# Row lists of the first two experts made from the ranks, ahead of the rest of the routing

## The reference

```python
def hier_moe(h, w_rg, b_rg, w_re, b_re, w_gate, w_up, w_down):
    t = h.reshape(b * s, d)
    p_group = jax.nn.softmax((t @ w_rg + b_rg).astype(F32), axis=-1)
    pg_top, g_top = lax.top_k(p_group, 1)                     # 1 of 4 groups
    ...
    pe_top, e_top = lax.top_k(p_exp, EXPERT_TOP_K)            # 2 of the 4 experts in it
    pe_top = pe_top / jnp.sum(pe_top, axis=-1, keepdims=True)
    ...
    for gi in range(N_EXPERT_GROUPS):
        hid = jax.nn.silu(jnp.einsum('nd,edf->nef', t, w_gate[gi])) * jnp.einsum('nd,edf->nef', t, w_up[gi])
        y = y + jnp.einsum('nef,efd->nd', hid * combine[:, gi, :, None], w_down[gi])
```

## Time and profile before

| | |
|---|---|
| median of 3 runs | 825.15 us |
| lowest of them | 824.24 us |
| profiled execution, its own time | 824.05 us |
| its span, first to last instruction | 822.1 us |
| mean granted TensorE clock | 0.917 of 2.4 GHz |
| TensorE busy | 679.0 us, 83% of the span |
| VectorE busy | 333.1 us, 41% |
| ScalarE busy | 180.4 us, 22% |
| GpSimd busy | 134.4 us, 16% |
| moved by DMA | 178.26 MB, mean 217 GB/s |

### The profile page before, as it was taken

One profiled execution on the slowest core, in us unless ns is written; L12 is line 12 of the kernel. 1 busy time (PEld: TensorE's weight loads), 2 busy tenths in 40 slices (PEclk: granted clock), 3 DMA queues, 4 the chain that ended last, 5 costly groups with the idle time before them and its releaser, 6 DMA issues.

```text
span 822.1 us, 9279 instructions
## 1 busy us (share of the span) xinstructions
PE 679.0 (83%) x3561; PEld 393.8 (48%) x3565; DVE 333.1 (41%) x752; ACT 180.4 (22%) x434; POOL 134.4 (16%) x176
## 2 busy tenths in 40 slices
PE   0469899999999998889998922999999979999610
PEld 0455445667675797556554522444454434333200
DVE  4932475867567433767312257011211121112007
ACT  3203324122121213446311121111121120111003
POOL 8670022304041273000000001000000000000021
PEclk9769999999999998989999955899999998999865
DMA  9899902222220303540331296189999999999945
GB/s 333 270 309 281 365 17 103 103 103 103 103 103 1 54 1 121 171 172 2 136 120 52 107 389 223 58 279 330 390 389 391 399 387 399 371 380 397 406 130 228
DMA packets 89631, 178.26 MB, mean 217 GB/s; under 512 B 19602, under 2 KB 24300, under 8 KB 89580
## 3 DMA queue, kind: packets, MB, share of 16 engines
q1 hardware_dynamic: 79152, 155.31, 52.8%
q0 software_dynamic: 4544, 16.26, 6.0%
q10 hardware_dynamic: 5884, 6.00, 2.2%
HBM read 159.20 MB, written 18.35 MB: 216 GB/s over the span
## 4 chain that ended last, share of the span: by engine, by line
PE 64%; DVE 15%; DMA 8%; SPq 6%; ACT 3%; issue 2%; POOL 1%; POOLq 0%; ACTq 0%; DVEq 0%
PE ps L1003 11%; PE ps L1114 7%; PE ps L2168 6%; DMA gu<-in_w_up 6%; PE ps L2135 5%; PE ps L1034 4%; SPq L887 3%; PE ps L997 3%; DVE acc L1794 3%; PE ps L2246 2%; PE ps L2252 2%; PE ps L2132 2%; SPq L890 2%; PE ps L1029 2%; PE ps L2159 2%
## 5 line engine op out<-in xcount | busy, mean ns | idle before, releaser
L1003 PE MATMUL ps<-gu,xgT 128*128 128x512 f32 x256 | 116.5, 615 | 9.1 <-DMA gu<-in_w_up 6.5
L1003 PEld LDWEIGHTS ps<-gu,xgT 128*128 128x128 f32 x256 | 49.9, 198 | 71.9 <-issue 64.6
L1460 POOL DMA_INDIRECT xg<-xn_rows,list x16 | 14.9, 932 | 400.2 <-PE ps L972 210.0
L2168 PE MATMUL ps<-hT,winr 128*128 128x512 f32 x144 | 72.5, 612 | 0.2
L1794 DVE SCALAR_TENSOR_TENSOR acc<-ada,st,acc 128x512 f32<-128x512 f32 x84 | 68.1, 811 | 2.3
L1034 PE MATMUL ps<-dn,hidT 128*128 128x512 f32 x128 | 56.5, 594 | 0.0
L1114 PE MATMUL ps<-wout,yT 128*128 128x512 f32 x128 | 55.9, 595 | 0.0
L1082 DVE TENSOR_TENSOR hidm<-sg,ps 128x512 f32<-128x512 f32 x8 | 5.5, 688 | 120.8 <-ACT sg L1050 120.8
L1648 POOL TENSOR_TENSOR cc<-low,lev 128x512 f32<-128x512 f32 x20 | 30.2, 1519 | 129.7 <-DVE low L1980 104.2
L997 PE MATMUL ps<-gu,xgT 128*32 128x256 f32 (+1 forms) x384 | 45.2, 464 | 7.2 <-DMA gu<-in_w_up 7.2
L2135 PE MATMUL ps<-hT,wind 128*128 128x512 f32 x96 | 42.3, 593 | 0.0
(11 more groups left out here) (405 smaller groups left out, 1039.7 us busy)
## 6 DMA issues: line engine op xcount, KB each, us to landing
gu<-in_w_gate SPq DMA_DIRECT2D x16, 2048.0 KB, 18.8
gu<-in_w_up SPq DMA_DIRECT2D x16, 2048.0 KB, 23.5
dn<-in_w_down SPq DMA_DIRECT2D x16, 2048.0 KB, 21.0
ada<-in_w_ada SPq DMA_DIRECT2D x12, 2048.0 KB, 10.0
expert_rows<-zero POOLq DMA_DIRECT2D x12, 512.0 KB, 12.3
expert_rows<-yo ACTq DMA_DIRECT2D x8, 512.0 KB
wout<-in_w_out SPq DMA_DIRECT2D x1, 3072.0 KB, 10.9
x<-in_x SPq DMA_DIRECT2D x2, 1024.0 KB, 6.3
```

Of the source, the lines that this page charges most:

```text
L1003: ins = nc.tensor.matmul(PS[2 * b + w][:, :], T["xgT"][:, k, :], w_in[:, w, k, :], start=(k == 0), stop=(k == KT - 1))
L2168: ins = t.matmul(bank[:, :], w(k), T["hT"][:, k, :], start=(k == 0), stop=(k == KT - 1))
```

## The change

It makes the row lists of experts 0 and 1 in another way, and moves work around them.

- As soon as `rank` is copied, `r16 = (rank + 1) * chosen` is made, and from it, for each of experts 0 and 1, one one-hot matrix of all four token blocks at once (128 x 512 elements; the row number plus 1 equals r16). Four products with one column each (the token's number) per expert make the list. This takes place after the rank products on TensorE and in front of the copy of `count` on DVE.
- DVE copies the two columns of the list behind `order` (the new step `first_list`), and does the block that makes `experts` straight after it. Then comes the rest of the chain as before, up to `r16` (now written over).
- POOL starts on step `first_list`, not `list`; the wait for `list` comes before the gather of expert 2.
- TensorE does rows 0 and gate and up 0 before the 16 list products, and these write to another bank, PS[5], at columns 64 to 91. A wait for `list` stands before down 0, which writes that bank too.
- DVE does `dve_rows(0)` in the middle of the chain (behind line 1366), then the rest of the places, then waits for the 16 list products, copies the list, and does the product of expert 0 and `dve_rows(1)`. The weights w1, w2 and the list of the extra places come after that.

The whole diff:

```diff
--- before.py
+++ after.py
@@ -48,8 +48,9 @@
 FT = F // P
 EXTRA = 12
 NBUF = 3
-ROUTING = {"chosen": 1, "places": 2, "slots": 3, "list": 4, "experts": 5, "w12": 6, "route_i": 7}
-ROUTING_PE = {"rank_mm": 1, "list_mm": 2}
+ROUTING = {"chosen": 1, "first_rows": 2, "second_rows": 3, "first_list": 4, "experts": 5, "places": 6, "slots": 7,
+           "list": 8, "w12": 9, "route_i": 10}
+ROUTING_PE = {"rank_mm": 1, "first_list_mm": 2, "list_mm": 3}
 SIZES = [128] * 8 + [64] * 4 + [32] * 4
 TILE_START = [sum(SIZES[:n]) for n in range(E + 1)]
 TILE_START += [TILE_START[E] + P * (n + 1) for n in range(EXTRA - 1)]
@@ -1175,16 +1176,21 @@
                            start=False, stop=(i == ST))
         ins.then_inc(sem("routing_pe"), 1)
 
+        for e in range(2):
+            pe.wait_ge(sem("routing"), ROUTING[("first_rows", "second_rows")[e]])
+            for i in range(ST):
+                ins = t.matmul(PS[5][:, e:e + 1], T["in_row"][:, e, i, :], T["tok"][:, i:i + 1], start=(i == 0),
+                               stop=(i == ST - 1))
+        ins.then_inc(sem("routing_pe"), 1)
+
+        pe_rows(pe, 0, 0, 16)
+        pe_gate_up(pe, 0, 0)
         pe.wait_ge(sem("routing"), ROUTING["places"])
         for n in range(2):
             for i in range(ST):
-                ins = t.matmul(PS[6][:, P:P + E + EXTRA], T["in_row"][:, n, i, :], T["in_tile"][:, n, i, :],
+                ins = t.matmul(PS[5][:, 64:64 + E + EXTRA], T["in_row"][:, n, i, :], T["in_tile"][:, n, i, :],
                                start=(n + i == 0), stop=(n == 1 and i == ST - 1))
         ins.then_inc(sem("routing_pe"), 1)
-
-        pe.wait_ge(sem("routing"), ROUTING["list"])
-        pe_rows(pe, 0, 0, 16)
-        pe_gate_up(pe, 0, 0)
         pe_rows(pe, 1, 1, 16)
         for n in range(1, E):
             b = n % 2
@@ -1192,6 +1198,8 @@
             pe_gate_up(pe, n, b)
             if n + 1 < E:
                 pe_rows(pe, n + 1, 1 - b, 16 * ((n + 1) // 2 + 1))
+            if n == 1:
+                pe.wait_ge(sem("routing"), ROUTING["list"])
             pe_down(pe, n - 1)
         pe_hidden(pe, E - 1, 1)
         pe_down(pe, E - 1)
@@ -1327,12 +1335,27 @@
         dve.wait_ge(sem("routing_pe"), ROUTING_PE["rank_mm"])
         rank, cnt, xe, t16, incl, bb = (T[n][:] for n in ("rank", "count", "xe", "t16", "incl", "bb"))
         link(v.tensor_copy(rank, PS[6][:, 0:ST * E].rearrange("p (i e) -> p i e", i=ST)))
+        r16 = T["r16"][:]
+        link(v.scalar_tensor_tensor(r16, rank, 1.0, T["chosen"][:, 0:ST], ALU.add, ALU.mult))
+        for e in range(2):
+            v.scalar_tensor_tensor(T["in_row"][:, e], T["row_n"][:].unsqueeze(1).broadcast_to([P, ST, P]), 1.0,
+                                   r16[:, :, e:e + 1].broadcast_to([P, ST, P]), ALU.add,
+                                   ALU.is_equal).then_inc(sem("routing"), 1)
         link(v.tensor_copy(cnt, PS[6][:, ST * E:(ST + 1) * E]))
         key, versus, order, pad, tile0 = (T[n][:] for n in ("key", "versus", "size", "pad", "tile0"))
         link(v.scalar_tensor_tensor(key, cnt, float(E), T["pinned"][:], ALU.mult, ALU.add))
         link(v.tensor_tensor(versus, key.unsqueeze(1).broadcast_to([P, E, E]), key.unsqueeze(2).broadcast_to([P, E, E]),
                              ALU.is_gt))
         link(v.tensor_reduce(order, versus, AX.X, ALU.add))
+        dve.wait_ge(sem("routing_pe"), ROUTING_PE["first_list_mm"])
+        v.tensor_copy(T["list"][:, 0:2], PS[5][:, 0:2]).then_inc(sem("routing"), 1)
+        e1 = T["e1"][:]
+        link(v.tensor_tensor(versus, order.unsqueeze(1).broadcast_to([P, E, E]), e1.unsqueeze(2).broadcast_to([P, E, E]),
+                             ALU.is_equal))
+        link(v.tensor_tensor(versus, versus, e1.unsqueeze(1).broadcast_to([P, E, E]), ALU.mult))
+        link(v.tensor_reduce(T["rf"][:, 1 + EXTRA:1 + EXTRA + E], versus, AX.X, ALU.add))
+        v.tensor_copy(T["route_i"][:, 1 + EXTRA:1 + EXTRA + E],
+                      T["rf"][:, 1 + EXTRA:1 + EXTRA + E]).then_inc(sem("routing"), 1)
         link(v.tensor_scalar(tile0, order, float(P), None, ALU.mult))
         for m, n in enumerate(STEPS_DOWN):
             less = float(SIZES[n - 1] - SIZES[n])
@@ -1358,12 +1381,14 @@
         link(v.scalar_tensor_tensor(e16[:], e16[:], float(P), wide_pad, ALU.is_ge, ALU.mult))
         link(v.tensor_tensor(rank, rank, e16[:], ALU.add))
 
-        r16 = T["r16"][:]
         link(v.tensor_scalar(e16[:], rank, float(P), None, ALU.is_ge))
         link(v.scalar_tensor_tensor(r16, e16[:], -float(P), rank, ALU.mult, ALU.add))
         for m in (2, 3, 4):
             link(v.tensor_scalar(T["s16"][:], rank, float(m * P), None, ALU.is_ge))
             link(v.scalar_tensor_tensor(r16, T["s16"][:], -float(P), r16, ALU.mult, ALU.add))
+        v.memset(T["yo"][:, 0:1], 0.0).then_inc(sem("yo_d"), 1)
+        v.memset(T["yo"][:, 1:2], 0.0).then_inc(sem("yo_st"), 16)
+        dve_rows(dve, 0)
         link(v.tensor_tensor(e16[:], e16[:], bb.unsqueeze(1).broadcast_to([P, ST, E]), ALU.mult))
         link(v.tensor_tensor(e16[:], e16[:], rank, ALU.add))
         link(v.tensor_tensor(e16[:], e16[:], tile0.unsqueeze(1).broadcast_to([P, ST, E]), ALU.add))
@@ -1382,14 +1407,9 @@
         ins.then_inc(sem("routing"), 1)
         v.tensor_copy(T["slot"][:], T["slotf"][:]).then_inc(sem("routing"), 1)
         dve.wait_ge(sem("routing_pe"), ROUTING_PE["list_mm"])
-        v.tensor_copy(T["list"][:], PS[6][:, P:P + E + EXTRA]).then_inc(sem("routing"), 1)
-        e1 = T["e1"][:]
-        link(v.tensor_tensor(versus, order.unsqueeze(1).broadcast_to([P, E, E]), e1.unsqueeze(2).broadcast_to([P, E, E]),
-                             ALU.is_equal))
-        link(v.tensor_tensor(versus, versus, e1.unsqueeze(1).broadcast_to([P, E, E]), ALU.mult))
-        link(v.tensor_reduce(T["rf"][:, 1 + EXTRA:1 + EXTRA + E], versus, AX.X, ALU.add))
-        v.tensor_copy(T["route_i"][:, 1 + EXTRA:1 + EXTRA + E],
-                      T["rf"][:, 1 + EXTRA:1 + EXTRA + E]).then_inc(sem("routing"), 1)
+        v.tensor_copy(T["list"][:, 2:E + EXTRA], PS[5][:, 66:64 + E + EXTRA]).then_inc(sem("routing"), 1)
+        dve_product(dve, 0, 0)
+        dve_rows(dve, 1)
         w1, w2, ed = T["w1t"][:], T["w2t"][:], T["ed"][:]
         dve.wait_ge(sem("exp_out"), 1)
         link(v.tensor_reduce(w1, T["eg"][:], AX.X, ALU.add))
@@ -1404,13 +1424,6 @@
             link(v.tensor_reduce(T["rf"][:, 1 + x:2 + x], t16, AX.X, ALU.add))
         link(v.tensor_scalar(T["rf"][:, 1:1 + EXTRA], T["rf"][:, 1:1 + EXTRA], float(E - 1), None, ALU.min))
         v.tensor_copy(T["route_i"][:, 0:1 + EXTRA], T["rf"][:, 0:1 + EXTRA]).then_inc(sem("routing"), 1)
-
-
-        v.memset(T["yo"][:, 0:1], 0.0).then_inc(sem("yo_d"), 1)
-        v.memset(T["yo"][:, 1:2], 0.0).then_inc(sem("yo_st"), 16)
-        dve_rows(dve, 0)
-        dve_product(dve, 0, 0)
-        dve_rows(dve, 1)
         for n in range(1, E):
             dve_product(dve, n, n % 2)
             if n + 1 < E:
@@ -1449,7 +1462,7 @@
     def pool_moe(pool):
         g = nc.gpsimd
         at = bass.IndirectOffsetOnAxis
-        pool.wait_ge(sem("routing"), ROUTING["list"])
+        pool.wait_ge(sem("routing"), ROUTING["first_list"])
         for b in range(2):
             pool.wait_ge(sem(f"xn2_st{b}"), 32)
 
@@ -1461,6 +1474,8 @@
                                  at(ap=T["list"][0:m, slot:slot + 1], axis=0)).then_inc(sem(f"xg_in{b}"), 16)
 
         for n in range(E):
+            if n == 2:
+                pool.wait_ge(sem("routing"), ROUTING["list"])
             if n >= 2:
 
                 pool.wait_ge(sem("xg_tr"), n - 1)
```

## The result

The changed kernel takes 813.52 us in the median of 4 runs (811.59 to 815.48); the kernel before took 824.69 beside it, in the median of 4, of which one of 1769.59 stands alone and is not in the ratio. The ratio is 0.987, with a 95% interval of 0.984 to 0.990: 1.3% faster. The forecast was 814.9, and a change within 2% of before. The profiled execution took 813.66, its span is 811.8 (822.1 before). The lines in its rows are those of the changed kernel, 1 to 15 higher than before for the same statement.

What follows compares the result with a forecast made beforehand. Balanced DMA and TensorE from 551 to 790 hang on products of experts 0 and 1: 11.5 us sooner minus a 1.8 detour gives 9.7, so 814.35, plus half of 1.1 for the median: 814.9 us; range 811 to 818.5.

Steps and rivals of the forecast that it cites:

- What the end hangs on: Full stage from 551 to 790: products and weight loads start from products of experts 0 and 1; everything behind 9.7 us sooner.
- the rival with a chance of 0.05: Full DMA stage bound by something not starting with products 0 and 1, so the end stays, 824.6; chance 0.05.
- From `rank` to the gather: Steps from the copy of rank to the first gather's issue: at 489.55 instead of 505.13, 15.58 us sooner.
- 8 products of one column: TensorE's early list products, priced at 0.226 us each: four from 486.66 and four more, ending at 488.46.
- one-column products take over 2 us: Sign of being wrong, for the early list products on TensorE ahead of the first gather.
- The landing: First gather, issued while expert 2's weights come in: takes 8.5 us, landing at 498.05; bounds 4.2 and 9.0.
- the estimate of 5.5: First gather's landing if queues take turns: half the rate, 1.3 us more than alone, 5.5 us; not used in the sum.
- DVE ready: DVE's chain ahead of row copies 0 ends at 497.2; the later one only if the gather takes under about 5.5.
- the rival: First gather lands fast, in 4.2 us; DVE is then the bound, gain 12.8, time 811.8 us; chance 0.12.
- Products 0: Gate and up products of expert 0: start at 501.85, 11.5 us sooner, and again take 16.82 at a half-clock start.
- The detour: List products, transposes and row copies between products 0 and 1: 4.6 us instead of 2.8, costing 1.8.
- The clock's fall: Rival: clock falls between products 0 and 1, costing 2.2 us, up to 2.9; time 817.1 us; chance 0.22.

Runs made afterwards that it cites:

- e9_tail_ahead: Changed kernel with DVE's weights w1, w2 and list of extra places put back ahead of the row copies of expert 1; 821.3 us.
- e2_late_load3: Changed kernel with SP issuing expert 3's gate and up loads only behind the products of expert 1; 820.66 us.
- e1_one_list: Changed kernel with expert 0's list finished, copied and gathered on its own, expert 1's behind it in another PSUM bank; 813.42 us.
- e3_quiet: Changed kernel with SP holding expert 2's loads until the first gather has landed; 811.48 us.
- e5_lists_only: Changed kernel with early lists kept, but the 16 list products again ahead of rows 0 and DVE copying rows 0 behind the whole list; 822.29 us.
- e4: Changed kernel with the 16 list products done twice between the products of experts 0 and 1; 816.77 us.
- e6: Changed kernel with the 16 list products behind the transposes of rows 1, and DVE's list copy behind the rows of expert 1; 815.89 us.
- e11: Changed kernel with list products behind the transposes of rows 1, run again in rounds; median 812.51 us, 0.986 of before.
- e10_changed: The changed kernel once more, unaltered, in rounds on one chip; median 814.57 us, 0.988 of before.

## Why the prediction was right

The mechanism stood, and the sum was within 1.4 us of the measured median. That it came so near is in part luck, since terms of it were off in opposite directions. By its steps:

- **What the end hangs on: right.** The start of products 1 moved by 10.97 us, the chain at 634 by 10.96, the span by 10.3; the sum had 9.7. Over the kernels of the table the end follows the start of products 1 (for e9_tail_ahead with its 2.5 us of slower products) one to one within 2 us, but for e2_late_load3, where the loads were parted from the products: there the end moved by 7.6 with products 1 in place. The gain was not given back, the rival with a chance of 0.05.
- **From `rank` to the gather: mis-sized.** The step "8 products of one column" took 3.58 us, not 1.8. A float32 product shows as two records: the 16 records of line 1181 are 8 products in the code (`for n in range(2)`, `for i in range(ST)`), and so 0.226 us is the price of a record and 0.45 that of a product. The prediction read 16 records as 16 products and then priced 8 products by records. The text ahead of it reads the same way: the 16 products of line 1181 are 8 in the code, and the 32 gate and up products of a full expert are 16 (8 blocks of the model's width, two matrices). By the prediction's own sign, "one-column products take over 2 us", this step was wrong. The gather was issued 13.8 sooner than before, not 15.6. e1_one_list showed it: with only the first 8 records ahead of it the list copy came 1.7 sooner. The one-hot matrices were right: 1.29 for the two, 1.3 forecast.
- **The landing: mis-sized the other way.** 7.2, not 8.5; it was inside the bounds. e3_quiet shows that the weights of expert 2 cause the rise over 4.2, and e5, e2 and e1 show 7.2, 7.3 and 7.5 for the same place. The Trainium skill ("DMA: Bandwidth & Descriptors", Queues, rings and completion order) has the engines take turns between queues; the estimate of 5.5 made from it does not agree with the trace, whose rise of 3.0 over the 4.2 is about twice the estimate's 1.3.
- **DVE ready: right in kind, closer in size.** The list came 1.8 us later than forecast, and its chain ended at 499.4, not 497.2. The transposes ended at 500.5, so it was still hidden; with the fast gather it was the bound, as the rival said.
- **Products 0: 15.56, not 16.82.** The clock rose sooner behind their start at 502.15 than behind 513.34 in the kernel before (windows as in the earlier trace rows, the changed kernel and then the kernel before):

```profile
505.00:506.00 1.00, 1.00 (x4) 0.40 (x3) 1.00 (x6) 0.00 (x0) 0.00 (x0) 0.82 0.02 8
```

```profile
519.00:520.00 1.00, 1.00 (x3) 0.38 (x2) 0.00 (x0) 0.00 (x0) 0.00 (x0) 0.96 0.00 0
```

  That it rose sooner is chance, as far as the profiles tell, and not the change. In the seven profiles whose code is the same up to here (the changed kernel twice, e2, e4, e6, e9, e11) the set took 15.43 to 16.46 us, and e5_lists_only, with TensorE's order of the kernel before, took 15.41 where that kernel took 16.82. So 1.3 us of the profile's 11.0 can't be put down to the change. The Trainium skill ("TensorE: Matmul & The Clock Gate", Part 1) has the monitor run on its own time, and the trace agrees: the same work behind nearly the same idle time took different times in different executions.
- **The detour: 1.5, not 1.8**, since DVE's product and the hidden transposes lay beside other work.
- **The clock's fall: didn't come**, with 4.3 us in 5 profiles of that length, nor with 6.0. With 5.8 us more of idle time in e9_tail_ahead it came. But narrow work is not shown to be safe: in all 13 profiles the clock fell between 4 and 6 us after the last dense products of the output projection (0.64 at 471 in the earlier trace rows, 0.93 at 475 in e10_changed, where these products ended 4 us later), with TensorE busy at narrow products but for a wait of 1.2 us, or two. Whether such waits, which stand there like the 1.18 of the earlier trace rows, make the difference to the stretch between experts 0 and 1 was not tried. So the rival's 0.22 was not unreasonable, and its cause stays open.

Against the 9.7 forecast, products 1 started 11.0 sooner: 1.8 was lost at the list, and 1.3 was won at the landing, 0.2 at the row copies, 1.3 at products 0 and 0.3 at the detour. Without the chance at products 0 it would have been 9.7 to the tenth, which is luck too, since the other terms cancel. In the second round, e10_changed, the medians differ by 9.7 as well (824.23 and 814.57). Behind products 1 the profile gave back 0.7, and the forecast had added 0.55 to the profiled time for the median, where the median was 0.1 below it.

## What to carry to other kernels

Where a long chain of small instructions stands ahead of a stage that is full, ask which few numbers the first item of that stage really needs, make these first, and let the rest run beside the first products; but do both, since the early numbers alone bought next to nothing. Look at the second bound (here DVE's chain, and the transfer that now meets a full queue) together with the first. And before a price per record is used for instructions counted in the code, hold one line's records against its loop.

## What the runs showed of the hardware

- A float32 product of 128x128 by 1 column costs TensorE as much as one by 28: 16 records in 3.58 and 3.61 us at half clock. In bfloat16 four such products of two columns took 0.27 us at the same clock, where four float32 ones take 1.8.
- Between experts 0 and 1, 6.0 us of narrow products and transposes with 1.0 us of waiting at their end kept the full clock, and a gap of 6.8 us without any lost it. After the output projection narrow products with a wait or two of 1.2 us lost it within 4 to 6 us, in each of 13 profiles.
- The same 32 records of gate and up products behind nearly the same idle time took 15.43 to 16.46 us in seven profiles, by when the clock rose, and 13.9 to 14.0 at the full clock.
- The first gather of 512 KB took 4.2 to 4.6 us with expert 2's 6 MB of loads not in its way, and 7.2 to 8.0 beside them.
- With loads of 4 MB issued at once behind others, SP stood 11.45 us in one issue (e2_late_load3).
